# Mixer input projection in the first of two blocks: compression units get a tile pair of their own, weight splits are issued one unit earlier

## What is computed

```python
for l in range(DEPTH):                      # DEPTH = 2
    mod = (cond @ ada_w[l] + ada_b[l]).reshape(B, N_SUBLAYERS, 3, 1, D)
    h = adaln_pre(x, norm_g[l, 0], mod[:, 0, 0], mod[:, 0, 1])
    x = x + 0.5 * mod[:, 0, 2] * swiglu(h, ffn1_w13[l], ffn1_w2[l])
    h = adaln_pre(x, norm_g[l, 1], mod[:, 1, 0], mod[:, 1, 1])
    p = dict(zip(names, jnp.split(h @ w_in[l] + b_in[l], splits, axis=-1)))
    y_a = nsa_mixer(...)                    # attention, with compressed keys and values
    y_b = short_conv_mixer(...)
    y_c = gated_deltanet(...)
    y_d = mlstm_mixer(...)
    y = jnp.concatenate([rms_norm(y_a, ...), rms_norm(y_b, ...), y_c, y_d], axis=-1)
    x = x + mod[:, 1, 2] * (y @ w_out[l])
    ...                                     # the second swiglu sublayer

def compress(kv, w1, w2):                   # inside nsa_mixer, for keys and for values
    blocks = jnp.concatenate([ch[:, :-1], ch[:, 1:]], axis=2) + cmp_pos
    hid = jax.nn.silu(blocks.reshape(B, nc, CMP_BLOCK * dh) @ w1)
    return hid @ w2
```

## Time and profile before

| | us |
|---|---|
| three runs | 3592.55, 3593.41, 3593.98 |
| median | 3593.41 |
| profiled execution, its time | 3595.14 |
| its span, first to last instruction | 3593.2 |
| TensorE busy | 3420.8 (95%) |
| VectorE busy | 1970.3 (55%) |
| ScalarE busy | 1138.6 (32%) |

### The profile page before, as it was taken

The page is one execution under the profiler, slowest core; times in us unless marked ns, Lnnn a source line. Parts: engine busy times, 40 slices in busy tenths (PEclk is TensorE's granted clock), DMA queues, the critical chain, the costliest instruction groups (busy, mean ns, idle before and its releaser), DMA issues.

```text
span 3593.2 us, 47374 instructions
## 1 busy us (share of the span) xinstructions
PE 3420.8 (95%) x17388; PEld 2756.9 (77%) x17388; DVE 1970.3 (55%) x3028; ACT 1138.6 (32%) x1687; POOL 347.4 (10%) x298
## 2 busy tenths in 40 slices
PE   7999998989999999999897999999899999989999
PEld 5888766777888788876677788876778887668887
DVE  6663446666652466344666665446666624756642
ACT  4222334433221222233442322233343313343321
POOL 1000100141000100010014100011100011120002
PEclk9999999989999999999998999999999999999999
DMA  8553222104543355322210354321223332122332
GB/s 320 196 180 103 86 77 77 42 11 142 188 133 107 124 193 188 107 87 68 81 45 6 131 197 136 107 85 59 66 82 99 104 103 70 57 67 94 99 104 83
DMA packets 100385, 386.48 MB, mean 108 GB/s; under 512 B 11086, under 2 KB 12238, under 8 KB 99624
## 3 DMA queue, kind: packets, MB, share of 16 engines
q1 hardware_dynamic: 100264, 384.82, 32.5%
HBM read 382.65 MB, written 2.12 MB: 107 GB/s over the span
## 4 chain that ended last, share of the span: by engine, by line
PE 87%; DVE 7%; ACT 3%; issue 2%; DMA 1%; POOL 1%; SPq 0%; ACTq 0%; DVEq 0%; POOLq 0%
PE bank L2786 19%; PE bank L2788 19%; PE bank L2787 19%; PE bank L2891 4%; PE bank L2893 4%; PE bank L2892 4%; PE bank L2797 1%; PE bank L2798 1%; PE bank L2799 1%; ACT wH L1092 1%; DVE wL L1610 1%; PE bank L2979 1%; DMA ada<-in_ada_first 1%; PE bank L3248 1%; PE bank L2996 1%
## 5 line engine op out<-in xcount | busy, mean ns | idle before, releaser
L1092 ACT ACTIVATE wH<-wR 128x1024 fp32r<-128x1024 f32 (+2 forms) x489 | 545.5, 1116 | 1730.1 <-PE bank L2788 1382.6
L1610 DVE TENSOR_TENSOR wL<-wR,wH 128x1024 fp32r<-128x1024 f32 (+2 forms) x489 | 645.0, 1319 | 704.8 <-ACT wH L1092 704.6
L2786 PE MATMUL bank<-hH,wH 128*128 128x512 f32 x2048 | 796.8, 389 | 0.4 <-DVE wL L1610 0.4
L2787 PE MATMUL bank<-hH,wL 128*128 128x512 f32 x2048 | 796.7, 389 | 0.0
L2788 PE MATMUL bank<-hL,wH 128*128 128x512 f32 x2048 | 796.7, 389 | 0.0
L2786 PEld LDWEIGHTS bank<-hH,wH 128*128 128x128 f32 x2048 | 384.4, 188 | 80.5 <-DVE wL L1610 0.8
L2788 PEld LDWEIGHTS bank<-hL,wH 128*128 128x128 f32 x2048 | 384.4, 188 | 80.0
L2787 PEld LDWEIGHTS bank<-hH,wL 128*128 128x128 f32 x2048 | 384.4, 188 | 79.8
L2788 PE MATMUL bank<-gL,wH 128*128 128x512 f32 x1056 | 410.8, 389 | 0.0
L2786 PE MATMUL bank<-gH,wH 128*128 128x512 f32 x1056 | 410.8, 389 | 0.0
L2787 PE MATMUL bank<-gH,wL 128*128 128x512 f32 x1056 | 410.8, 389 | 0.0
(11 more groups left out here) (442 smaller groups left out, 4055.8 us busy)
## 6 DMA issues: line engine op xcount, KB each, us to landing
wR<-in_ffn_w SPq DMA_DIRECT2D x176, 512.0 KB, 3.6
adaw<-in_ada_w SPq DMA_DIRECT2D x144, 512.0 KB, 4.2
wR<-in_ffn_w SPq DMA_DIRECT2D x64, 704.0 KB, 4.1
wR<-in_w_up SPq DMA_DIRECT2D x88, 512.0 KB, 3.5
wR<-in_w_mix SPq DMA_DIRECT2D x76, 512.0 KB, 3.5
wR<-in_w_down SPq DMA_DIRECT2D x32, 704.0 KB, 4.1
wR<-in_w_in SPq DMA_DIRECT2D x40, 512.0 KB, 3.5
wR<-in_w_out SPq DMA_DIRECT2D x16, 512.0 KB, 3.5
```

What stands on the lines that cost most here:

```text
L1092: act.activation(wH[n][:, 0:tiles, :], wR[n][:, 0:tiles, :], ACT.Copy).then_inc(S.w_hi, 1)
L1610: dve.tensor_tensor(wL[n][:, 0:tiles, :], wR[n][:, 0:tiles, :], wH[n][:, 0:tiles, :].bitcast(F32), ALU.subtract).then_inc(S.w_lo, 1)
L2786: pe.matmul(o, wH[n][:, k, :], rH[:, r, :], start=start and k == 0, stop=False)
L2787: pe.matmul(o, wL[n][:, k, :], rH[:, r, :], start=False, stop=False)
```

## The change

1. **Buffers.** From position 12 to 27 the compression units use the third pair (`buffer(p)` is 2), and the column units 13, 15, ... 27 take pairs 0 and 1 in turn. `freed(p)` is the earlier position that last used the pair of p. The raw buffers stay at p % 2, and SyncE's code is the same.
2. **Splits.** `split_at(p)` says at which quarter of p the split of p + 2 is issued: 1 for p = 10, 11, 13, 15, ... 25, and 3 elsewhere. `hi_in` and `lo_in` take the pair from `buffer` and wait for the unit `freed`.
3. **Norm steps.** `norm` and `norm_out` move to quarters 0 and 2 of units 13, 15, 17 and 19, one norm to a unit.

```diff
+def buffer(p):
+    if p < 12 or p >= 28:
+        return p % 2
+    return (p - 13) // 2 % 2 if p in UNIT else 2
+
+def freed(p):
+    if p < 12:
+        return p - 2
+    return max(v for v in range(2, p) if (buffer(v) if v > 2 else 2) == buffer(p))
+
+def split_at(p):
+    return 1 if 10 <= p < 26 and freed(p + 2) < p else 3
...
-    for n, a, b in ((0, (15, 0), (15, 2)), (1, (17, 0), (17, 2)), (2, (17, 3), (19, 0)), (3, (19, 1), (19, 2))):
+    for n, a, b in ((0, (13, 0), (13, 2)), (1, (15, 0), (15, 2)), (2, (17, 0), (17, 2)), (3, (19, 0), (19, 2))):
...
+            def hi_in(p, tiles):
+                act.wait_ge(S.w_in[p % 2], at(S.w_in[p % 2], 16 * ((U_IN + p) // 2 + 1)))
+                act.wait_ge(S.w_used, at(S.w_used, U_IN + freed(p) + 1))
+                high = (wH[0], wH[1], third[0])[buffer(p)]
+                act.activation(high[:, 0:tiles, :], wR[p % 2][:, 0:tiles, :], ACT.Copy).then_inc(S.w_hi, 1)
...
-                        if q == 3:
-                            hi(U_IN + p + 2, (U_IN + p + 2) // 2 + 1, KT if p + 2 < N_MIX else NE, p % 2)
+                        if q == split_at(p):
+                            hi_in(p + 2, KT if p + 2 < N_MIX else NE)
...
-                        if q == 3:
-                            if p in UNIT:
-                                keep(UNIT[p])
-                            lo(U_IN + p + 2, KT if p + 2 < N_MIX else NE, p % 2)
+                        if q == 3 and p in UNIT:
+                            keep(UNIT[p])
+                        if q == split_at(p):
+                            lo_in(p + 2, KT if p + 2 < N_MIX else NE)
...
-                    pe.matmul(o, x2, wH[n][:, 2 * t:2 * t + 2, :], start=j == 0 and t == 0, stop=False)
-                    mm = pe.matmul(o, x2, wL[n][:, 2 * t:2 * t + 2, :], start=False, stop=j == 3 and t == 3)
+                    pe.matmul(o, x2, third[0][:, 2 * t:2 * t + 2, :], start=j == 0 and t == 0, stop=False)
+                    mm = pe.matmul(o, x2, third[1][:, 2 * t:2 * t + 2, :], start=False, stop=j == 3 and t == 3)
```

More of the change, by code:

```diff
@@ L1610, in lo, with lo_in @@
                 dve.tensor_tensor(wL[n][:, 0:tiles, :], wR[n][:, 0:tiles, :], wH[n][:, 0:tiles, :].bitcast(F32),
+                                  ALU.subtract).then_inc(S.w_lo, 1)
+            def lo_in(p, tiles):
+                dve.wait_ge(S.w_hi, at(S.w_hi, U_IN + p + 1))
+                high, low = ((wH[0], wL[0]), (wH[1], wL[1]), third)[buffer(p)]
+                dve.tensor_tensor(low[:, 0:tiles, :], wR[p % 2][:, 0:tiles, :], high[:, 0:tiles, :].bitcast(F32),
                                   ALU.subtract).then_inc(S.w_lo, 1)
@@ L2904, in quarter_third, with compress @@
                     mm.then_inc(S.w_used, 1)
-            def compress(c, n):
+            def compress(c):
                 kv, j = c // 4, c % 4
@@ L3109, in mixers_in @@
                             else:
-                                quarter(bank[d % 2][:, :], p % 2, q)
+                                quarter(bank[d % 2][:, :], buffer(p), q)
                             steps(p, q)
                     else:
-                        compress((p - 12) // 2, p % 2)
+                        compress((p - 12) // 2)
                         steps(p, 3)
```

## The result

The changed kernel takes 3574.11 us (median of five runs) against 3593.69 us of the kernel before (six runs beside it). A sixth run of the changed kernel was in a slow state, 5430.98 us at a mean granted clock of 0.638; it is not counted (with it the median would be 3574.82). The ratio is 0.9945, with a 95% interval of 0.9934 to 0.9957: faster by 0.55%, some 20 us. Forecast were 3571.5 us, with a range of 3560 to 3582. The profiled execution took 3572.88 us with a span of 3571.0; the forecast for that pair was 3573.2 and 3571.3. So the total came out within 1 us for the profiled pair and within 3 us for the median.

The account below looks back on a forecast made before the run. TensorE, busy 95% of the span, was taken as the bound, so only its idle time and clock could be won. Gains of 11.9 us (first layer) and 10.0 (second), together 21.9, took the median from 3593.41 to 3571.5 us; range 3560 to 3582.

Parts of the forecast that it names:

- The waits for the low part: First column matmuls of units 13 to 27 waiting for their weights' low part: all seven go, 9.5 us a layer.
- the chain of the first attention step: Unit 21: step starts 5.04 us after compression unit 20, bound by unit 20, split of 22 and `d_out`; same in both.
- The norm steps: Unit 19's wait of 2.68 us for `norm_out` 2 goes with a norm to a unit; GpSimd's earlier squares cost 0.
- `d_turn`: New wait on `d_scale`, ready at T + 11.9 (T: end of unit 17), TensorE there at T + 7.8: 4.2 us.
- The shared port pair: Subtraction of 20 stands still behind GpSimd's square, the reduce behind it: `d_turn` waits 4.35 instead of 4.2, 0.3 in all.
- the sum's T + 4.8: Link before `d_turn`: GpSimd's square of the whole output, taking 2.81 us, ends 4.8 us after unit 17's end.
- Unit 27: TensorE's 1.53 us wait for a ScalarE copy: of the 1.26 won at the unit's start about 0.95 stay.
- The clock: Low level around units 13 to 19 goes, 5.2 and 3.3 us won; a fall behind `d_turn` costs 1.3 a layer.
- the second rival: Attention units give nothing: waits of 23 to 27 come back elsewhere, 3.8 us a layer lost, 3579; chance 0.19.
- the one of a small wait at `d_turn`: One chain link isn't in the way, so 4.2 and 1.3 go: 11 us more, 3560.5; chance 0.12.
- The one that the clock falls as often as before: Clock falls for other waits, so the term of 5.9 us goes: 3577.4; chance 0.10.
- The slower one: Clock stays low after the 4.2 us wait through units 21 to 27: 13.9 us slower, 3607; chance 0.04.

Follow-up runs that it names:

- `norms_only`: Kernel before with the norm steps alone at their new places, buffers and splits untouched: 3591.18 us, ratio 0.9990.
- `splits_only`: Changed kernel with the norm steps back at the old places, so buffers and splits alone: 3566.53 us, ratio 0.9921.
- `reduce_first`: Changed kernel with the reduce of the mLSTM squares ahead of the subtraction of unit 20 on VectorE, at (18, 3): 3570.27 us, ratio 0.9941.
- `scale_first`: Changed kernel with `d_scale` ahead of the subtraction of unit 21 on VectorE, at (19, 1): 3567.73 us, ratio 0.9925.

## Why the prediction was right, and where its terms were off

- **The waits for the low part: right.** All seven went, 9.5 us a layer, and the 0.55 of the score step with them. Unit 21's did run into the chain of the first attention step, whose wait is 1.56 in both kernels' first layer, and in the second 2.05 against 1.55. That the chain takes 5.04 us from the start of unit 20 didn't hold, though: it is 5.94 and 5.91, since the matmuls of unit 20 itself run at the low level of the clock, 0.21 us apart instead of 0.11.
- **The norm steps: right on the wait, incomplete on its worth.** The 2.68 went and no square came late. But `norms_only` and `splits_only` show that the two parts don't add: with early splits the old norm places would have cost a wait of 1.85 and spared 3.51. The prediction booked 2.68 to the norm steps and the new wait to the splits, when the norm steps' place is a cause of it as much: norm 3 stands on ScalarE ahead of the copy of 21 by that move.
- **`d_turn`: right, mis-sized by 0.7.** Forecast T + 11.9 and a wait of 4.2, measured T + 11.3 and 3.51. The term that failed is the 0.40 us from ScalarE's copy to VectorE. It was read from the bracket in the earlier trace rows, which is how long VectorE had sat idle since `keep`, not a hand-over; the copy of 21 ends at 543.70 and the subtraction starts at 543.73. Neighbours on one engine overlap by 0.1 as well, which the sum of durations left out.
- **The shared port pair: the rule right, the sum right by luck.** The subtraction of 20 took 2.73 us, begun 0.24 behind GpSimd's square, and ended 1.07 behind its end. By the Trainium skill (SBUF — State Buffer, "SBUF: two separate sides") the later of two such instructions stands still until the first is done. The estimate by this page was 0.15 us later than the sum's T + 4.8. The reduce started at T + 4.93, so the trace agrees, and `reduce_first` with it. That T + 4.8 came out so near is two errors that cancel: it has the square at 2.81, itself a held-up one, where it took 1.90, and no standstill of the subtraction, which ended 1.07 behind the square. With a square of 1.90 the forecast would have shown 1.0 us a layer to win.
- **Unit 27: 0.3 off.** Forecast to rise from 1.53 by 0.3; it rose to 2.19, as TensorE came 1.26 earlier and ScalarE only 0.6 to 0.7.
- **The clock: the mis-sized term.** Booked was 5.2 + 3.3 won and 2.6 lost again, 5.9. The one low stretch between 500 and 560 us came behind `d_turn`, as forecast, and its price there was about right: from the turn to the first attention step it is 7.0 and 7.5 us against 5.8 in the kernel before, 1.2 and 1.7 a layer where 1.3 was booked. Unit 27's was not booked. What was lost again in the profiled execution is 1.7 at `d_turn` in each layer and 1.7 in unit 27 of the first. The 8.5 won belongs to that one execution; two others of the same kernel had 5.2. So in the stretches read the clock gives 3.4 by the profiled pair (8.5 less 5.1). Over the whole span it gives nothing: the mean granted clock is 0.980 before and 0.979 after, as falls came and went elsewhere.
- **A term that was not booked: the passage into a unit.** It is the 0.27 us shown for unit 13, and the sum has nothing for it. At the starts of units 13, 15, 17, 19, 23, 25 and 27 it is 0.2 to 0.35 each, some 1.9 us a layer and 3.8 in all.
- **How the total came out.** The waits alone fell from 31.7 to 15.0 us (2 x 15.8 against 7.3 and 7.7), which is 16.7 where the forecast had 16.1. With 3.4 of the clock and 3.8 of the passages that is 23.9 in the stretches read. A check: from the start of unit 12 to that of unit 26 the two layers took 82.5 and 81.0 us and take 70.3 and 70.8, 22.4 less, where waits of 14.4, clock of 5.1 and passages of 3.3 give 22.8. The span fell by 22.2, so some 1.7 were lost again outside the stretches. That the profiled pair came out within 0.3 us is in part luck: a clock term 2.5 too large and the loss elsewhere stand against passages that were not booked.
- **The median** moved by 19.6 us and the profiled pair by 22.3. The difference is which executions were profiled: the one of the kernel before lies 1.5 above the median of its six, the one of the changed kernel 1.2 below that of its five. The forecast had assumed that both lie 1.7 above their medians. How much one execution differs from the next the two profiles of the changed kernel show: their spans are 3571.0 and 3573.8, and 3.0 us of that arise before unit 12 of the first layer starts (506.06 and 509.03).
- **The rivals.** No wait for VectorE came up in the attention units, so that the second rival fell; the one of a small wait at `d_turn` came true only once its order was changed (`scale_first`). The one that the clock falls as often as before, which takes the 5.9 away, did not hold in the stretches read (3.4 were won), but it describes the span as a whole. The slower one, a clock that stays low, was not seen: over 550 to 560 us it was back at 0.99.

## What to carry to other kernels

- Where short units stand between long ones, a split or a load that waits for the long unit before is late by its own length less the short one. Give the short units a buffer of their own and put the work ahead of the store that waits for TensorE. The buffer alone left 5.8 of 10.5 us of waits here.
- Work that is moved up in an in-order queue is put ahead of something. List what it passes on every engine that runs it, and follow the longest chain through those rows: here one subtraction ahead of one scaling took back 3.5 of 12.7 us a layer.
- Count a wait that goes as its idle time and a bit more: here some 0.27 us at each.
- Sum the waits that go apart from the clock. Waits repeat to 0.1 us from one execution to the next, the clock's losses around them don't, and one profile can't price them.

## What the runs showed of the hardware that was not expected

- With the same waits of 2.1 to 2.7 us, the low level of TensorE's clock took 8.5, 5.2 and 5.2 us of work in three executions of one kernel, and none in a stretch with three such waits of another, whose second layer lost 3.3. It came behind 7 of 18 waits of 2.13 us, behind six of six of 2.7 and with eight of eight of 3.5.
- A wait cost TensorE more than the idle time in its row. With the wait of 2.13 us gone, unit 13's second matmul came 2.41 us sooner after the start of compression unit 12: 1.14 us instead of 3.55.
- A VectorE subtraction and a GpSimd square that meet don't slow each other down by a share: the later one stands still. With the square first, VectorE took 2.73 us instead of 1.22. With VectorE first it is the other way about, as in the kernel with late splits, where the square of 1.04 us took 1.95, and the 0.28 us step of VectorE after it 1.13, held in its turn:

```profile
508.29 1.22 DVE L1643 TENSOR_TENSOR wL<-wR,wH 128x1024 fp32r<-128x1024 f32 x1
508.46 1.95 POOL L2658 TENSOR_TENSOR hf<-pm 128x512 f32<-128x512 f32 x1 [81.38 <-DVE pm L2118]
509.42 1.13 DVE L1962 TENSOR_TENSOR WD<-pm,cst 128x128 f32<-128x128 f32 x1
```
